# A normalisation chain in front of split-float32 matmuls, with its scale and its low parts moved to other engines

## The chip, the cores and the metric

The kernel runs on one core of one Trainium2 chip. The metric is the device time of one execution in microseconds, as the median of several runs.

## What is computed

The reference is two transformer blocks over 256 tokens with 256 context tokens and a model width of 1024, all in float32. Nearly every part begins with a root-mean-square norm, and in the first block the norm is modulated by a scale and a shift that come from a conditioning vector:

```python
def _rms_norm(x, gain):
    y = xf * lax.rsqrt(jnp.mean(xf * xf, axis=-1, keepdims=True) + EPS)
    return (y * gain.astype(jnp.float32)).astype(x.dtype)

def _modulated_norm(h, gain, shift, scale):
    return _rms_norm(h, gain) * (1.0 + scale) + shift

def _swiglu(h, w1, w2):
    a, b = jnp.split(h @ w1, 2, axis=-1)
    return (jax.nn.silu(a) * b) @ w2
```

The first block has two layers, each with an MLP, a mixer (delta rule, then window attention) and a second MLP, so it has six modulated norms. The second block has a plain norm with a gain in front of its three branches, one in front of its cross attention and one in front of its MLP.

## The kernel before

Everything is feature-major: a tile of 128 features lies across the partitions and the tokens lie along the free dimension (512 for context and latent tokens together, 256 for the latent ones alone). `KT` is 8, the number of feature tiles `d` of the model width.

A float32 product is made of three matmuls over split operands: weight and activation are each split into a high part (rounded to `fp32r`) and a low part (the rest), and `three` (lines 229 to 234) multiplies high by low (L232), low by high (L233) and high by high (L234) into one PSUM bank. Weights stream in units of eight 128x128 tiles: SyncE starts the load into one of three landing slots, ScalarE copies the high part (`feed_act`, L215), and GpSimd subtracts to get the low part (`feed_pool`, L225), both into one of four slots. TensorE waits for a unit's low part before its first tile.

The activations of a norm are split in the same way. The sum of squares is made on TensorE (L430), ScalarE takes the root (L459), VectorE the reciprocal `rr` (L493), and `spread_pe` (L470) spreads `rr` over the partitions into PSUM bank 5, followed by a fixed number of matmuls that nobody reads (`busy_pe`, L421: 14 rows in the trace for 512 tokens, 8 for 256). Then, for each feature tile `d`:

- VectorE, `norm_x_dve` (L499): work = residual x bank 5, all tokens in one instruction;
- ScalarE, `norm_act` (L486): high part = scale x work + shift, one instruction for each part of the tokens. A modulated norm over 512 tokens has two parts of 256, since context and latent tokens have their own scale and shift; every other norm has one part of 256;
- VectorE, `norm_z_dve` (L505): work = scale x work + shift, in place and in float32, by part, once the high part of that tile has been made (it overwrites what ScalarE reads);
- GpSimd, `norm_pool` (L521): low part = work - high part, all tokens in one instruction.

`norm_dve` interleaves the VectorE steps: it runs two tiles ahead with L499 and then alternates. The first matmuls of the next stage take the tiles in the order of `d`: `linear` waits for the low part of tile `d` and then runs `first` output tiles on it (two in an MLP, so six matmuls for each `d`; four in the second block's `glu` and `up2`, so twelve). The order on every engine is written out by hand in `pe_program`, `act_program`, `dve_program` and `pool_program`; each engine runs its list in order, and an instruction waits on a counter of another engine (`PE`, `AC`, `DV`, `PO`).

The norms are called, in order: `norm00` (before `mlp00`, at the start of the kernel, where L499 runs before the modulation scale has been made), `norm01` (before the delta projections), `norm02` (before `mlp01`), `norm10` (before `mlp10`), `norm11` (before the window-attention projections), all of these over 512 tokens; `norm12` (before `mlp11`) over 256 tokens; and `norm mix`, `norm xattn` and `norm mlp` of the second block, with a gain and without a shift. In an MLP the first L365 matmuls follow the two output tiles of `first`, so their start marks the end of the part of the matmuls that is fed by the norm.

## Time and profile before

| | |
|---|---|
| time, median of 3 runs | 2927.93 us (2921.97 to 2930.43) |
| the profiled execution: its own time | 2923.75 us |
| the profiled execution: its span | 2921.6 us |
| instructions | 51936 |
| TensorE busy | 2781.6 us, 95% of the span |
| VectorE busy | 1533.2 us, 52% |
| ScalarE busy | 1188.2 us, 41% |
| GpSimd busy | 1532.1 us, 52% |
| mean granted clock of TensorE | 0.978 |
| HBM read | 373.34 MB |

The span runs from the first to the last instruction of the profiled execution; the rest of its time, 2.15 us, lies around it. The profile's timeline merges instructions of one line that follow each other, so that a row's second number is the time from the start of the first to the end of the last of them. PE is TensorE, DVE is VectorE, ACT is ScalarE, POOL is GpSimd.

### The profile page before, as it was taken

The page shows a single profiled execution, that of the slowest core. Times are in us where ns is not written, and L with a number is a line of the kernel's source. Part 1 is how long each engine was busy: PE and PEld are TensorE (multiplying, and loading weights), DVE is VectorE, ACT ScalarE, POOL GpSimd, SP SyncE. Part 2 cuts the span into 40 slices and gives each one's busy share as a digit, 9 for nine tenths or more (in the row PEclk, how much of TensorE's full clock was granted, in tenths as well). Part 3 has the DMA queues.
Part 4 walks back from the last instruction along what each step waited for, and adds up shares of the span by engine and source line. Part 5 has one row for each costly group of instructions (what it writes and reads, how often), then busy time and mean ns, then how long its engine had stood idle before and what let it go on. Part 6 is the DMA issues. An engine that isn't in the chain of part 4 may idle for free.

```text
span 2921.6 us, 51936 instructions
## 1 busy us (share of the span) xinstructions
PE 2781.6 (95%) x21510; PEld 2393.9 (82%) x21510; DVE 1533.2 (52%) x2800; ACT 1188.2 (41%) x2083; POOL 1532.1 (52%) x857
## 2 busy tenths in 40 slices
PE   7999999988889999999999998899998999998999
PEld 5888877767777788887888885799997888997999
DVE  3777236645554666416665136453285765723570
ACT  3222235434453322223222245544455465545553
POOL 4444444443324544445444451488883665686797
PEclk8999999999999999999999999999998999999999
DMA  6565323210001555323554326265552433353365
GB/s 256 191 214 188 109 66 101 89 59 3 4 3 51 177 174 182 130 95 132 189 174 162 96 81 116 73 195 189 170 191 95 131 124 117 115 166 123 130 193 162
DMA packets 105969, 380.89 MB, mean 130 GB/s; under 512 B 11367, under 2 KB 16648, under 8 KB 104456
## 3 DMA queue, kind: packets, MB, share of 16 engines
q1 hardware_dynamic: 87304, 310.47, 33.0%
q10 hardware_dynamic: 18432, 67.12, 6.6%
q8 instruction: 171, 2.80, 0.4%
q14 instruction: 62, 0.51, 0.1%
HBM read 373.34 MB, written 4.19 MB: 129 GB/s over the span
## 4 chain that ended last, share of the span: by engine, by line
PE 84%; DVE 6%; POOL 3%; ACT 3%; issue 2%; DMA 1%; SPq 0%; ACTq 0%; DVEq 0%
PE bank L232 23%; PE bank L233 23%; PE bank L234 23%; POOL weights_lo L225 2%; PE bank L828 1%; DVE norm_work L505 1%; PE upper_banks L232 1%; PE upper_banks L233 1%; PE upper_banks L234 1%; DVE norm_work L499 1%; DMA ada_first<-w_ada 1%; DVE square_sums L452 1%; PE upper_banks L1564 1%; PE bank L1555 1%; PE bank L925 1%
## 5 line engine op out<-in xcount | busy, mean ns | idle before, releaser
L225 POOL TENSOR_TENSOR weights_lo<-weights_landing,weights_hi 128x1024 fp32r<-128x1024 f32 x554 | 1336.8, 2419 | 1116.5 <-ACT weights_hi L215 1116.0
L215 ACT ACTIVATE weights_hi<-weights_landing 128x1024 fp32r<-128x1024 f32 x554 | 586.6, 1061 | 1223.8 <-PE bank L234 1099.8
L232 PE MATMUL bank<-normed_hi,weights_lo 128*128 128x512 f32 (+1 forms) x2664 | 912.7, 343 | 16.9 <-POOL normed_lo L521 11.8
L233 PE MATMUL bank<-normed_lo,weights_hi 128*128 128x512 f32 (+1 forms) x2664 | 902.8, 339 | 0.0
L234 PE MATMUL bank<-normed_hi,weights_hi 128*128 128x512 f32 (+1 forms) x2664 | 902.1, 339 | 0.0
L232 PEld LDWEIGHTS bank<-normed_hi,weights_lo 128*128 128x128 f32 x2664 | 504.6, 189 | 101.2 <-POOL normed_lo L521 27.1
L234 PEld LDWEIGHTS bank<-normed_hi,weights_hi 128*128 128x128 f32 x2664 | 504.4, 189 | 61.4
L233 PEld LDWEIGHTS bank<-normed_lo,weights_hi 128*128 128x128 f32 x2664 | 504.8, 189 | 59.4
L232 PE MATMUL bank<-hidden_hi,weights_lo 128*128 128x512 f32 (+1 forms) x960 | 329.6, 343 | 0.0
L233 PE MATMUL bank<-hidden_lo,weights_hi 128*128 128x512 f32 (+1 forms) x960 | 329.4, 343 | 0.0
L234 PE MATMUL bank<-hidden_hi,weights_hi 128*128 128x512 f32 (+1 forms) x960 | 328.8, 343 | 0.0
L573 DVE TENSOR_TENSOR hidden_lo<-silus,hidden_hi 128x512 fp32r<-128x512 f32 (+1 forms) x88 | 210.8, 2395 | 87.4 <-ACT hidden_hi L560 87.4
L626 DVE SCALAR_TENSOR_TENSOR residual<-bank,gate,residual 128x256 f32<-128x256 f32 x80 | 35.5, 479 | 358.4 <-PE bank L234 358.4
L234 PEld LDWEIGHTS bank<-hidden_hi,weights_hi 128*128 128x128 f32 x960 | 180.2, 188 | 24.3
L233 PEld LDWEIGHTS bank<-hidden_lo,weights_hi 128*128 128x128 f32 x960 | 180.2, 188 | 24.2
L232 PEld LDWEIGHTS bank<-hidden_hi,weights_lo 128*128 128x128 f32 x960 | 180.1, 188 | 24.2
L391 DVE CUSTOM_DVE_ANT_0 ada_products<-ada_rows,upper_banks,k_cond_pack 128x1024 f32<-128x1024 f32 x128 | 163.3, 1276 | 21.0 <-DMA ada_rows<-w_ada_rows 11.8
L391 DVE CUSTOM_DVE_ANT_0 ada_rows<-ada_rows,upper_banks,k_cond_pack 128x1024 f32<-128x1024 f32 x128 | 163.1, 1274 | 0.0
L571 DVE TENSOR_TENSOR silus<-silus,bank 128x512 f32<-128x512 f32 (+1 forms) x88 | 54.6, 621 | 185.5 <-PE bank L234 160.5
L1746 DVE SCALAR_TENSOR_TENSOR upper_banks<-gl,k_pack,upper_banks 128x255 f32<-128x255 f32 (+14 forms) x240 | 113.5, 473 | 8.2
L521 POOL TENSOR_TENSOR normed_lo<-norm_work,normed_hi 128x512 fp32r<-128x512 f32 (+1 forms) x72 | 76.7, 1069 | 77.3 <-DVE norm_work L505 77.0
L452 DVE TENSOR_TENSOR square_sums<-square_sums,squares 128x512 f32<-128x512 f32 (+1 forms) x48 | 67.2, 1400 | 36.0 <-ACT squares L444 36.0
(442 smaller groups left out, 3800.9 us busy)
## 6 DMA issues: line engine op xcount, KB each, us to landing
weights_landing<-w_up SPq DMA_DIRECT2D x176, 512.0 KB, 3.5
ada_rows<-w_ada_rows ACTq DMA_DIRECT2D x128, 512.0 KB, 4.3
weights_landing<-w_down SPq DMA_DIRECT2D x88, 512.0 KB, 3.5
weights_landing<-w_dn SPq DMA_DIRECT2D x33, 512.0 KB, 3.4
weights_landing<-w_mlp_up SPq DMA_DIRECT2D x32, 512.0 KB, 3.5
weights_landing<-w_mlp_down SPq DMA_DIRECT2D x32, 512.0 KB, 3.5
weights_landing<-w_gate SPq DMA_DIRECT2D x24, 512.0 KB, 3.4
weights_landing<-w_xbc SPq DMA_DIRECT2D x24, 512.0 KB, 3.5
```

The source lines that it names most:

```text
L215: k.nc.scalar.activation(k.WH[:, u % SLOTS, :], k.W[:, u % LANDS, :], ACT.Copy).then_inc(*k.AC.mark(("unit hi", u)))
L225: k.nc.gpsimd.tensor_tensor(k.WL[:, u % SLOTS, :], k.W[:, u % LANDS, :], k.WH[:, u % SLOTS, :].bitcast(F32), ALU.subtract).then_inc(*k.PO. ...
L232: nc.tensor.matmul(out, ll, rh, start=start, stop=False, skip_group_check=True)
L233: nc.tensor.matmul(out, lh, rl, start=False, stop=False, skip_group_check=True)
L234: return nc.tensor.matmul(out, lh, rh, start=False, stop=stop, skip_group_check=True)
L391: nc.vector.tensor_tensor_reduce(k.row[r % ROW_LANDS][:] if c else k.row_out[:], k.row[r % ROW_LANDS][:], k.upper[:, c * D:(c + 1) * D], 1 ...
L452: k.nc.vector.tensor_tensor(s, s, k.sq[:, d % 2, 0:tokens], ALU.add).then_inc(*k.DV.mark((st, "sum", d)))
L521: k.nc.gpsimd.tensor_tensor(lo(d), work(d), hi(d).bitcast(F32), ALU.subtract).then_inc(*k.PO.mark((st, "lo", d)))
L571: nc.vector.tensor_tensor(s, s, k.B[(2 * p + 1) % 4][:, 0:tokens], ALU.mult).then_inc(*k.DV.mark((st, "raw", p)))
L573: nc.vector.tensor_tensor(lo(p), s, hi(p).bitcast(F32), ALU.subtract).then_inc(*k.DV.mark((st, "lo", p)))
L626: nc.vector.scalar_tensor_tensor(x, k.B[n % 4][:, a - first:b - first], gate(n, c), x, ALU.mult, ALU.add).then_inc(*k.DV.mark(*([(st, "ev" ...
L1746: nc.vector.scalar_tensor_tensor(y[:, a:LAT], x[:, 0:LAT - a], w[:, at, j:j + 1], y[:, a:LAT], ALU.mult, ALU.add).then_inc(*k.DV.mark(("co ...
```

## The change

In every norm the scale moves from the second and third step into the first: `norm_scaled_dve` (L498 of the changed kernel) makes work = (residual x scale) x bank 5 with one `scalar_tensor_tensor` for each part of the tokens. ScalarE makes the high part as work + shift, one part as soon as that part of work is there. The in-place step L505 of before is gone.

In the six modulated norms VectorE makes the low part too (`norm_low_dve`, L505 of the changed kernel): low = (work + shift) - high, by part, again one `scalar_tensor_tensor`, and the matmuls wait for VectorE (`norm_ready`). GpSimd only waits there until the last low part is made, and then goes on with its weights. In the three norms of the second block GpSimd still makes the low part, and now waits for ScalarE's high part alone. `norm_dve` now runs one tile ahead instead of two. In `norm00` all steps come after the scale.

```diff
-def norm_act(k, act, st, work, hi, parts, when=None):
+def norm_act(k, act, st, work, hi, parts):
     for d in range(KT):
-        act.wait_ge(*k.DV.after(st, "x", d))
         for n, (a, b, scale, shift) in enumerate(parts):
-            k.nc.scalar.activation(hi(d)[:, a:b], work(d)[:, a:b], ACT.Identity, scale=scale(d),
-                                   bias=shift(d) if shift else 0.0).then_inc(*k.AC.mark(*([(st, "hi", d)] if n == len(parts) - 1 else [])))
+            act.wait_ge(*k.DV.after(st, "scaled", d, n))
+            k.nc.scalar.activation(hi(d)[:, a:b], work(d)[:, a:b], ACT.Identity,
+                                   bias=shift(d) if shift else 0.0).then_inc(*k.AC.mark((st, "hi", d, n)))
...
-def norm_x_dve(k, dve, st, d, src, work, tokens, bank=5):
+def norm_scaled_dve(k, dve, st, d, src, work, parts, bank=5):
     if d == 0:
         dve.wait_ge(*k.PE.after(st, "spread"))
-    k.nc.vector.tensor_tensor(work(d), src(d), k.B[bank][:, 0:tokens], ALU.mult).then_inc(*k.DV.mark((st, "x", d)))
-def norm_z_dve(k, dve, st, d, work, parts):
-    dve.wait_ge(*k.AC.after(st, "hi", d))
     for n, (a, b, scale, shift) in enumerate(parts):
-        k.nc.vector.tensor_scalar(work(d)[:, a:b], work(d)[:, a:b], scale(d), shift(d) if shift else None, ALU.mult,
-                                  *((ALU.add,) if shift else ())).then_inc(*k.DV.mark(*([(st, "z", d)] if n == len(parts) - 1 else [])))
+        k.nc.vector.scalar_tensor_tensor(work(d)[:, a:b], src(d)[:, a:b], scale(d), k.B[bank][:, a:b], ALU.mult,
+                                         ALU.mult).then_inc(*k.DV.mark((st, "scaled", d, n)))
+def norm_low_dve(k, dve, st, d, work, hi, lo, parts):
+    for n, (a, b, scale, shift) in enumerate(parts):
+        dve.wait_ge(*k.AC.after(st, "hi", d, n))
+        k.nc.vector.scalar_tensor_tensor(lo(d)[:, a:b], work(d)[:, a:b], shift(d), hi(d)[:, a:b].bitcast(F32), ALU.add,
+                                         ALU.subtract).then_inc(*k.DV.mark(*([(st, "lo", d)] if n == len(parts) - 1 else [])))
...
     norm_r_dve(k, dve, st, tokens)
-    for d in range(KT + 2):
+    for d in range(KT + 1):
         if d < KT:
-            norm_x_dve(k, dve, st, d, src, work, tokens, bank)
-        if d >= 2:
-            norm_z_dve(k, dve, st, d - 2, work, parts)
+            norm_scaled_dve(k, dve, st, d, src, work, parts)
+        if d and st in MODULATED:
+            norm_low_dve(k, dve, st, d - 1, work, hi, lo, parts)
+MODULATED = ("norm00", "norm01", "norm02", "norm10", "norm11", "norm12")
+def norm_ready(k, st):
+    return lambda d: (k.DV if st in MODULATED else k.PO).after(st, "lo", d)
 def norm_pool(k, pool, st, work, hi, lo):
+    if st in MODULATED:
+        pool.wait_ge(*k.DV.after(st, "lo", KT - 1))
+        return
     for d in range(KT):
-        pool.wait_ge(*k.DV.after(st, "z", d))
+        pool.wait_ge(*k.AC.after(st, "hi", d, 0))
         k.nc.gpsimd.tensor_tensor(lo(d), work(d), hi(d).bitcast(F32), ALU.subtract).then_inc(*k.PO.mark((st, "lo", d)))
...
     norm_r_dve(k, dve, "norm00", TOK)
     ada_dve(k, dve, 1)
-    for d in range(KT):
-        norm_x_dve(k, dve, "norm00", d, src, work, TOK)
     for u in range(2, ADA_FIRST):
         ada_dve(k, dve, u)
+    dve.wait_ge(*k.DV.after("ada scale", 0, 0))
     for d in range(KT):
-        norm_z_dve(k, dve, "norm00", d, work, modulated(k, 0, 0))
+        norm_scaled_dve(k, dve, "norm00", d, src, work, modulated(k, 0, 0))
+        if d:
+            norm_low_dve(k, dve, "norm00", d - 1, work, hi, lo, modulated(k, 0, 0))
+    norm_low_dve(k, dve, "norm00", KT - 1, work, hi, lo, modulated(k, 0, 0))
```

The order of VectorE's instructions at the beginning of `norm01`, before:

```order
L493 RECIPROCAL rr<-rms 128x4 [waits act_done]
L499 TENSOR_TENSOR norm_work<-residual,upper_banks 128x512 [waits pe_done]
L499 TENSOR_TENSOR norm_work<-residual,upper_banks 128x512 x2
L505 TENSOR_SCALAR norm_work<-norm_work,scale,mod 128x256 [waits act_done]
L505 TENSOR_SCALAR norm_work<-norm_work,scale,mod 128x256
L499 TENSOR_TENSOR norm_work<-residual,upper_banks 128x512
L505 TENSOR_SCALAR norm_work<-norm_work,scale,mod 128x256 [waits act_done]
```

and of the changed kernel at the same place (`norm_work`, `normed_hi` and `normed_lo` hold work, high and low part; x2, x3 are repeats):

```order
L491 RECIPROCAL rr<-rms 128x4 [waits act_done]
L498 SCALAR_TENSOR_TENSOR norm_work<-residual,scale,upper_banks 128x256 [waits pe_done]
L498 SCALAR_TENSOR_TENSOR norm_work<-residual,scale,upper_banks 128x256 x3
L505 SCALAR_TENSOR_TENSOR normed_lo<-norm_work,mod,normed_hi 128x256 [waits act_done] x2
L498 SCALAR_TENSOR_TENSOR norm_work<-residual,scale,upper_banks 128x256 x2
```

The last three rows of before (one L499 on 512 tokens, two L505) repeat until the eighth tile; in the changed kernel the last two rows (two L505, two L498) do. Four L498 now stand ahead of the first low part, and both halves of it wait for ScalarE.

At the start of the kernel VectorE's order around `norm00` was (L346 makes the scale of the first norm, L571 is the first instruction of `mlp00`):

```order
L493 RECIPROCAL rr<-rms 128x4
L499 TENSOR_TENSOR norm_work<-residual,upper_banks 128x512 x8
L332 TENSOR_TENSOR mod<-upper_banks,k_cond_pack 128x2x4x2 x2
L346 SCALAR_TENSOR_TENSOR scale<-mod,k_cond_pack 128x16
L505 TENSOR_SCALAR norm_work<-norm_work,scale,mod 128x256 x16
L571 TENSOR_TENSOR silus<-silus,bank 128x512
```

and is now:

```order
L491 RECIPROCAL rr<-rms 128x4
L332 TENSOR_TENSOR mod<-upper_banks,k_cond_pack 128x2x4x2 x2
L346 SCALAR_TENSOR_TENSOR scale<-mod,k_cond_pack 128x16
L498 SCALAR_TENSOR_TENSOR norm_work<-residual,scale,upper_banks 128x256 x4
L505 SCALAR_TENSOR_TENSOR normed_lo<-norm_work,mod,normed_hi 128x256 x2
L498 SCALAR_TENSOR_TENSOR norm_work<-residual,scale,upper_banks 128x256 x2
```

The eight products of L499 stood ahead of the scale; the products of L498 need it and stand behind it.

## Rows read from the trace of the kernel before

**Rows 1.** The page: busy time of each engine, and the ended-last chain by line

```profile
PE 2781.6 (95%) x21510; PEld 2393.9 (82%) x21510; DVE 1533.2 (52%) x2800; ACT 1188.2 (41%) x2083; POOL 1532.1 (52%) x857
...
PE bank L232 23%; PE bank L233 23%; PE bank L234 23%; POOL weights_lo L225 2%; PE bank L828 1%; DVE norm_work L505 1%; PE upper_banks L232 1%; PE upper_banks L233 1%; PE upper_banks L234 1%; DVE norm_work L499 1%; DMA ada_first<-w_ada 1%; D
```

**Rows 2.** Windows: us, then busy time (and count) by engine, PEclk, DMA share, GB/s

```profile
940.00:959.00 19.00, 16.84 (x68) 11.57 (x68) 15.23 (x25) 10.33 (x18) 12.17 (x9) 1.00 0.00 1
959.00:1322.00 363.00, 362.69 (x1572) 291.81 (x1571) 180.44 (x229) 97.47 (x118) 156.63 (x66) 1.00 0.46 154
```

**Rows 3.** Timeline of VectorE in norm02: start us, us, engine, line, operation

```profile
940.93 1.88 DVE L499 TENSOR_TENSOR norm_work<-residual,upper_banks 128x512 f32<-128x512 f32 x3 [0.74 <-PE upper_banks L470]
...
942.79 0.73 DVE L505 TENSOR_SCALAR norm_work<-norm_work,scale,mod 128x256 f32<-128x256 f32 x2
...
944.04 1.31 DVE L505 TENSOR_SCALAR norm_work<-norm_work,scale,mod 128x256 f32<-128x256 f32 x2
...
945.86 1.33 DVE L505 TENSOR_SCALAR norm_work<-norm_work,scale,mod 128x256 f32<-128x256 f32 x2
```

**Rows 4.** Timeline of TensorE in norm02

```profile
940.73 3.19 PE L421 MATMUL upper_banks<-k_cond_pack 128*128 128x256 f32 x14
...
944.93 0.50 PE L232 MATMUL bank<-normed_hi,weights_lo 128*128 128x512 f32 x1 [1.01 <-POOL normed_lo L521]
...
957.41 0.50 PE L232 MATMUL bank<-normed_hi,weights_lo 128*128 128x512 f32 x1
...
958.91 1.91 PE L365 MATMUL upper_banks<-k_cond_pack,cond 128*128 128x128 f32 x16
```

**Rows 5.** Timeline of GpSimd in norm02

```profile
943.60 1.27 POOL L521 TENSOR_TENSOR normed_lo<-norm_work,normed_hi 128x512 fp32r<-128x512 f32 x1 [8.68 <-DVE norm_work L505]
```

**Rows 6.** Groups by line and shape: count | busy us, mean ns of one | idle before

```profile
L2269 DVE SCALAR_TENSOR_TENSOR mem<-mem,k_pack,upper_banks 128x256 f32<-128x256 f32 x8 | 3.2, 470 | 0.0
...
L499 DVE TENSOR_TENSOR norm_work<-residual,upper_banks 128x512 f32<-128x512 f32 x40 | 25.9, 679 | 3.9 <-PE upper_banks L470 3.9
...
L499 DVE TENSOR_TENSOR norm_work<-residual,upper_banks 128x256 f32<-128x256 f32 x32 | 12.5, 412 | 6.2 <-PE upper_banks L470 6.2
...
L486 ACT ACTIVATE normed_hi<-norm_work,mod,scale 128x256 fp32r<-128x256 f32 x88 | 46.2, 591 | 21.1 <-DVE norm_work L499 19.6 <-DVE scale L346 1.5
...
L486 ACT ACTIVATE normed_hi<-norm_work,k_pack 128x256 fp32r<-128x256 f32 x24 | 11.5, 506 | 9.7 <-DVE norm_work L499 9.7
...
L779 DVE SCALAR_TENSOR_TENSOR dn_g<-dn_ab_tmp,k_pack 128x64 f32<-128x64 f32 x1 | 0.2, 227 | 0.0
...
L772 DVE TENSOR_TENSOR dn_ab_tmp<-upper_banks,k_pack 128x64 f32<-128x64 f32 x1 | 0.2, 215 | 0.0
...
L2258 DVE TENSOR_TENSOR ssd_y_lo<-ssd_xbc,ssd_y_hi 128x256 fp32r<-128x256 f32 x16 | 14.6, 920 | 0.7 <-ACT ssd_y_hi L2237 0.6
```

**Rows 7.** Timelines of ScalarE and TensorE around norm00

```profile
38.02 7.98 ACT L486 ACTIVATE normed_hi<-norm_work,mod,scale 128x256 fp32r<-128x256 f32 x16 [1.54 <-DVE scale L346]
...
41.28 0.80 PE L232 MATMUL bank<-normed_hi,weights_lo 128*128 128x512 f32 x1 [3.72 <-POOL normed_lo L521]
...
54.37 1.91 PE L365 MATMUL upper_banks<-k_cond_pack,cond 128*128 128x128 f32 x16
```

**Rows 8.** Timelines of VectorE and TensorE in norm12: its first product, first matmul after

```profile
1880.31 1.08 DVE L499 TENSOR_TENSOR norm_work<-residual,upper_banks 128x256 f32<-128x256 f32 x3 [0.78 <-PE upper_banks L470]
...
1889.86 0.28 PE L232 MATMUL bank<-normed_hi,weights_lo 128*128 128x256 f32 x1
```

**Rows 9.** Timelines of TensorE in norm mix, and of GpSimd and TensorE around norm xattn

```profile
2074.72 0.39 PE L232 MATMUL bank<-normed_hi,weights_lo 128*128 128x256 f32 x1 [0.52 <-POOL normed_lo L521]
...
2637.80 0.74 POOL L521 TENSOR_TENSOR normed_lo<-norm_work,normed_hi 128x256 fp32r<-128x256 f32 x1 [0.23 <-DVE norm_work L505]
...
2644.82 7.05 POOL L225 TENSOR_TENSOR weights_lo<-weights_landing,weights_hi 128x1024 fp32r<-128x1024 f32 x3
...
2647.22 0.50 PE L232 MATMUL bank<-weights_hi,mem_lo 128*128 128x512 f32 x1 [2.39 <-POOL weights_lo L225]
```

More of the change, by code:

```diff
@@ L691, in delta_pe @@
     linear(k, pe, st, "w_dn", DN_TILES, KT, lambda d: (k.n_hi[:, d, :], k.n_lo[:, d, :]), TOK, freed,
-           lambda d: k.PO.after("norm01", "lo", d), first=2, beside=beside)
+           norm_ready(k, "norm01"), first=2, beside=beside)
 def delta_act(k, act):
@@ L1760, in glu_pe @@
     freed = lambda n: None if n < 8 else k.AC.after("glu", "sig", (n - 8) // 2) if n % 2 else k.DV.after("glu", "ev", (n - 8) // 2)
-    linear(k, pe, "glu", "w_glu", 2 * KT, KT, both2(k), LAT, freed, lambda d: k.PO.after("norm mix", "lo", d), first=4, banks=8)
+    linear(k, pe, "glu", "w_glu", 2 * KT, KT, both2(k), LAT, freed, norm_ready(k, "norm mix"), first=4, banks=8)
 def glu_act(k, act):
@@ L2519, in mlp2_pe @@
     freed = lambda n: k.DV.after("up2", "square", n - 8) if n >= 8 else None
-    linear(k, pe, "up2", "w_mlp_up", 4 * KT, KT, both2(k), LAT, freed, lambda d: k.PO.after("norm mlp", "lo", d), first=4, banks=8)
+    linear(k, pe, "up2", "w_mlp_up", 4 * KT, KT, both2(k), LAT, freed, norm_ready(k, "norm mlp"), first=4, banks=8)
     out_pe(k, pe, "down2", "w_mlp_down", 4 * KT, lambda d: (k.mh_hi[:, d, :], k.mh_lo[:, d, :]), LAT,
@@ L2675, in pe_program @@
     spread_pe(k, pe, "norm11", TOK)
-    window_project_pe(k, pe, swa, lambda d: k.PO.after("norm11", "lo", d), lambda n: None)
+    window_project_pe(k, pe, swa, norm_ready(k, "norm11"), lambda n: None)
     window_heads_pe(k, pe, swa)
@@ L2701, in pe_program, with norm_of_act @@
     mlp2_pe(k, pe)
-def norm_of_act(k, act, st, tokens, where, parts, when=None):
+def norm_of_act(k, act, st, tokens, where, parts):
     src, work, hi, lo = where
     rms_act(k, act, st, tokens)
-    norm_act(k, act, st, work, hi, parts, when)
+    norm_act(k, act, st, work, hi, parts)
 def act_program(k, act):
@@ L2712, in act_program @@
     start_act(k, act)
-    norm_act(k, act, "norm00", *first_norm(k, TOK)[1:3], modulated(k, 0, 0), k.DV.after("ada scale", 0, 0))
+    norm_act(k, act, "norm00", *first_norm(k, TOK)[1:3], modulated(k, 0, 0))
     mlp_act(k, act, "mlp00")
@@ L2750, in norm_of_dve @@
     src, work, hi, lo = where
-    norm_dve(k, dve, st, src, work, tokens, parts)
+    norm_dve(k, dve, st, src, work, hi, lo, tokens, parts)
 def dve_program(k, dve):
```

8 lines of the change are left out of this document (3 added, 5 removed).

## The prediction

> **What bounds the kernel now.** I read the page first. TensorE is busy for 95% of the span, and the chain that ended last is mostly its matmuls L232, L233 and L234; of the norms, L505 and L499 of VectorE appear in it with 1% each [rows 1]. So time can only be won where TensorE waits, and the next view, the busy time by windows, shows where: in the 363 us of `mlp01` TensorE is busy for 362.69, in the 19 us of the norm ahead of it for 16.84, much of that in matmuls that nobody reads [rows 2]. Both stretches have a granted clock of 1.00, which is the upper level, 2.4 GHz. The MLP's rate gives the price of a matmul on 512 tokens: 362.69 / 1572 = 0.231 us, so 1.4 us for the six that each feature tile feeds.
>
> The timelines of the three engines in `norm02` show what paces the feeding. I count from the first L499, at 940.93. VectorE runs three products in 1.88 us (0.60 from start to start), then two L505 in 0.73, and once GpSimd works beside it two L505 in 1.31 [rows 3]. One tile, a product and two L505, then takes VectorE 1.82 us (945.86 - 944.04) [rows 3], more than the 1.4 us of its matmuls. The filler matmuls end at 943.92 (2.99 after the start), the first low part at 944.87, and TensorE starts on it at 944.93, 0.06 later; the eighth tile's six matmuls run from 957.41 to 958.91, 1.50 us with their wait [rows 4, 5]. From the first product to the end of the fed part it is 17.98 us. `norm01`, `norm10` and `norm11` repeat this pattern, three more times.
>
> **The change, part by part, in a norm over 512 tokens.** VectorE now issues 32 `scalar_tensor_tensor` on 256 tokens: 16 products and 16 low parts. L2269 is the same operation with a per-feature scalar and one input in PSUM: eight back to back took 3.2 us, so 0.40 us from start to start, and 0.47 for one [rows 6]. That is the product's price. No row shows the low part's form, two large inputs in SBUF and a scalar, on 256 elements. A two-input product L499 on 256 elements costs 0.34 from start to start (three in 1.08, one 0.41) [rows 6, 8]; a low part of 256 elements from two inputs, L2258, costs 0.92 on average [rows 6]. I take 0.40, since L779, a `scalar_tensor_tensor` with both inputs in SBUF on 64 elements, takes 227 ns where the plain sum L772 takes 215 [rows 6]: the kind of input adds next to nothing. The bounds are 0.34 and 0.92.
>
> With 0.40 for both, the first tile's low part is VectorE's sixth instruction and ends at 5 x 0.40 + 0.47 = 2.47 us, ahead of the fillers' end at 2.99. So TensorE starts at 3.0 instead of 4.0. Then VectorE gives a tile every 1.60 us, still above 1.4. The seventh tile's low part is the 30th instruction and ends at 29 x 0.40 + 0.47 = 12.07, the eighth's at 12.87. TensorE: 12.07 + 0.06 + 1.50 = 13.63, and 1.40 more for the eighth tile, which is ready: 15.03. Before it was 17.98, so a norm gains 2.95 us, and four gain **11.8 us**.
>
> ScalarE hides under this: one high part took 591 ns with scale and shift and 506 with a scale alone [rows 6]; with the shift alone I put it near 0.51, about 1.0 for a tile against VectorE's 1.60. The new waits of VectorE on each half are met: the high part of a tile is asked for after two further products. Behind such a wait stand the next tile's products, so a late ScalarE would stall everything; it has 0.6 us a tile to spare. GpSimd loses its eight low parts and waits instead; its next weights come at 12.9 instead of 16.4 after the first product, so nothing behind it (its low parts, and the loads that SyncE issues after them) is later.
>
> **norm00.** Its eight early products were hidden behind a wait for the scale; now they stand behind it. The first high part started at 38.02, the first matmul at 41.28, the fed part ended at 54.37 [rows 7]. Now the first product starts at 38.02, the first low part ends at 40.49, TensorE starts at 40.55, **0.7 us** earlier, and needs the same 13.09 us, since it is slower than VectorE here (last low part at 50.9).
>
> **norm12.** 256 tokens, one part. From first product to the end of the fed part: 1889.86 - 1880.31 = 9.55 [rows 8]. Now the first low part waits for product (0.47) and high part (0.51), with 0.05 at each handing over: it starts at 1.08. Each tile then takes 0.80, more than the 0.70 of its six half-size matmuls; the seventh low part ends at 6.35, TensorE needs 0.06 + 0.80 + 0.70 for the last two tiles: 7.91. The gain is **1.6 us**.
>
> **The three plain norms.** L505 goes out of the path. In `norm mix` TensorE waits 0.52 us for the first low part and is the slower one afterwards [rows 9]; a step of some 0.4 us leaves the chain, **0.4 us**, and the same in `norm mlp`, **0.4 us**. In `norm xattn` GpSimd's eight low parts take from 2637.80 to 2644.82, and TensorE stands still for 2.39 us until the weights behind them are split [rows 9]. Without the waits for L505 they take 8 x 0.74 = 5.92 and start 0.23 earlier: **1.3 us**.
>
> The sum is 11.8 + 0.7 + 1.6 + 0.4 + 0.4 + 1.3 = **16.2 us**. Against the profiled execution's 2923.75 (span 2921.6 and 2.15 around it) that makes 2907.6. The median of the runs shown is 4.2 above that execution, and the forecast is for a median: 2927.93 - 16.2 = **2911.7**. If the low part costs only 0.34, TensorE bounds the norms (2.99 + 8 x 1.40, and 0.2 for waits, 14.4), and the sum is 19.0.
>
> **Rivals.**
> *A: the low part streams at half rate.* One element costs (679 - 412) / 256 = 1.04 ns [rows 6], so 256 more of them make a low part 0.67. Then the eighth tile is ready at 16 x 0.40 + 15 x 0.67 + 0.74 = 17.19 and the part ends at 18.75, +0.77 in each of four norms; `norm00` becomes bound by VectorE and ends at 56.8, +2.4; `norm12` +0.2; the plain norms still give 2.1. Together +3.6: 2931.5. Against it: on 64 elements half rate would add 67 ns, and L779 is 12 above L772 [rows 6]. For it: that is one row, on few elements. Chance 0.12. The Trainium skill, Vector Engine (DVE) Microarchitecture Reference, section "Points that are easy to get wrong", states such a rule: "`S2S2D2_STT` with two non-bf16 SBUF sources halves throughput"; this is the form of every new low part. By that rule the time is this rival's.
> *B: the low part meets GpSimd.* If GpSimd worked on SBUF during the low parts, they would cost like L2258, 0.92. The norm turns into a loss from 0.62 on (16 x 0.40 + 16 x 0.62 + 1.6 = 17.98). At 0.92 the part ends at 22.7, +4.7 in four norms, +6.3 in `norm00`, +2.2 in `norm12`, less 2.1: +25.2, 2953.1. For it: L505 went from 0.73 to 1.31 a pair when GpSimd started [rows 3]. Against it: GpSimd had been idle for 8.68 us before its first low part [rows 5], and now it is told to wait until VectorE's last. Chance 0.05. The Trainium skill, SBUF — State Buffer, section "Who interferes with whom", says that a VectorE instruction with two SBUF inputs contends with a GpSimd instruction that reads SBUF; the new wait of GpSimd is what that rule asks for.
> *C: waits break VectorE's overlap.* If each low part, being behind a wait, starts only when the instruction before has ended, 16 starts lose 0.07 each. A 512-token norm then gains 1.9, `norm12` 1.1, the sum is 11.4: 2916.5. Against it: a round of before, with one wait in it, is the 0.60 of its product and some 1.24 of its L505 pair, with nothing left over [rows 3]. Chance 0.10.
>
> **How the numbers follow.** My forecast has 0.71, C 0.10, A 0.12, B 0.05, and 0.02 is for what I have not seen. A measurement of this kernel can tell 0.3%, 8.8 us, from no change. Forecast and C lie beyond that (16.2 and 11.4), with 0.04 taken off for a median that comes out high: faster 0.77. A is the same, with that 0.04 and part of the unseen: 0.18. B is slower: 0.05. The range runs from the lowest run shown less the largest sum, 2921.97 - 19.0 = 2903.0, to the highest run less C's sum without the plain norms, 2930.43 - 9.3 = 2921.1. It leaves out A and B.
>
> **What the profile of the changed kernel would show.** L498 and the new L505 at 0.47 us each or less, 0.40 from start to start; in `norm02` the filler rows run straight into the first L232, and L365 starts 15.0 us after the first product instead of 18.0; no idle time of L505 on ScalarE beyond the first tile of `norm12`; no L521 in the first block. L505 near 0.74 would be A, far above it with GpSimd busy B. I am wrong if L365 comes less than 1 us earlier, or if it does and the total does not follow, which would mean that a later stage waits for something that doesn't move with the norm.

## The result and the profile after

The changed kernel takes 2909.93 us (median of 6 executions, 2901.82 to 2913.49), the kernel before 2924.72 on the same chip (6 executions, 2919.43 to 2930.43). The ratio is 0.9946, with a 95% interval from 0.9927 to 0.9965: faster by 0.54%, some 15.8 us (the two medians lie 14.8 apart). 2911.7 was forecast, and a gain of 16.2. The profiled execution took 2910.77 us (span 2908.6), 13.0 less than that of before.

The page of the changed kernel, its first part (busy us, share of the span, instructions), and the chain that ended last by engine. These lines answer to [rows 1]:

```profile
PE 2787.6 (96%) x21510; PEld 2402.9 (83%) x21510; DVE 1497.4 (51%) x2816; ACT 1180.2 (41%) x2083; POOL 1473.1 (51%) x809
...
PE 87%; DVE 4%; POOL 3%; ACT 3%; issue 2%; DMA 1%; SPq 0%; ACTq 0%; DVEq 0%
```

TensorE's share goes from 95 to 96% with the same 21510 matmuls, and GpSimd has 48 instructions fewer, the low parts of six norms. L505 and L499, each 1% of the chain before, are gone from the part of the chain's list by line that the page prints.

Busy time by windows, of `norm02` and of `mlp01` behind it (us from the start, then busy us and instructions of each engine, granted clock of TensorE, DMA share, GB/s). They answer to [rows 2]:

```profile
935.00:954.00 19.00, 18.87 (x90) 14.49 (x89) 12.87 (x33) 11.96 (x22) 5.15 (x3) 1.00 0.09 27
954.00:1314.00 360.00, 359.69 (x1551) 289.03 (x1550) 180.00 (x229) 94.63 (x116) 153.49 (x64) 1.00 0.46 154
```

In 19 us TensorE is now busy for 18.87 instead of 16.84. Behind the norm nothing changed: 359.69 / 1551 = 0.232 us a matmul (0.231 before), and from the end of `norm02`'s fed part to the first product of `norm10` it is 364.42 us (364.41 before). So what the norm gave was not asked back by the MLP.

The timeline of `norm02` (start us, us, engine, line, operation). VectorE and ScalarE answer to [rows 3], TensorE and GpSimd to [rows 4, 5]:

```profile
935.88 3.19 PE L421 MATMUL upper_banks<-k_cond_pack 128*128 128x256 f32 x14
936.08 1.66 DVE L498 SCALAR_TENSOR_TENSOR norm_work<-residual,scale,upper_banks 128x256 f32<-128x256 f32 x4 [0.74 <-PE upper_banks L470]
...
939.23 0.88 DVE L505 SCALAR_TENSOR_TENSOR normed_lo<-norm_work,mod,normed_hi 128x256 fp32r<-128x256 f32 x2
940.02 0.87 DVE L498 SCALAR_TENSOR_TENSOR norm_work<-residual,scale,upper_banks 128x256 f32<-128x256 f32 x2
940.53 0.91 ACT L484 ACTIVATE normed_hi<-norm_work,mod 128x256 fp32r<-128x256 f32 x2 [0.67 <-DVE norm_work L498]
940.81 0.88 DVE L505 SCALAR_TENSOR_TENSOR normed_lo<-norm_work,mod,normed_hi 128x256 fp32r<-128x256 f32 x2
...
947.11 1.67 DVE L505 SCALAR_TENSOR_TENSOR normed_lo<-norm_work,mod,normed_hi 128x256 fp32r<-128x256 f32 x4
...
948.85 7.09 POOL L225 TENSOR_TENSOR weights_lo<-weights_landing,weights_hi 128x1024 fp32r<-128x1024 f32 x3 [18.78 <-DVE normed_lo L505]
950.95 1.91 PE L365 MATMUL upper_banks<-k_cond_pack,cond 128*128 128x128 f32 x16
```

VectorE runs without a gap, one tile every 1.58 us (940.81 - 939.23) instead of 1.82. ScalarE idles 0.67 us in each round and waits for the product, not the other way round. L365, the end of the fed part, comes 950.95 - 936.08 = 14.87 us after the first product instead of 17.98.

The groups of instructions that the prediction priced (busy us, mean ns of one, idle time before them and what ended it), which answer to [rows 6]:

```profile
L484 ACT ACTIVATE normed_hi<-norm_work,mod 128x256 fp32r<-128x256 f32 x88 | 39.8, 502 | 30.8 <-DVE norm_work L498 30.8
L505 DVE SCALAR_TENSOR_TENSOR normed_lo<-norm_work,mod,normed_hi 128x256 fp32r<-128x256 f32 x88 | 38.4, 479 | 0.4 <-ACT normed_hi L484 0.4
L498 DVE SCALAR_TENSOR_TENSOR norm_work<-residual,scale,upper_banks 128x256 f32<-128x256 f32 x88 | 38.0, 475 | 3.8 <-PE upper_banks L470 3.8
...
L484 ACT ACTIVATE normed_hi<-norm_work 128x256 fp32r<-128x256 f32 x24 | 8.9, 413 | 2.5 <-DVE norm_work L498 2.5
```

The low part, with two inputs in SBUF, costs 479 ns; the product, with one of them in PSUM, 475. Over all 88 low parts VectorE waited 0.4 us for ScalarE.

Laid side by side, the stretches from each norm's first product to the end of what it feeds (in `norm xattn`, to the end of the first unit of weights that it feeds; in `norm00`, from the start of L346, which makes the scale, to L365):

| stretch | before, us | predicted gain | after, us | gain |
|---|---|---|---|---|
| norm01, 02, 10, 11 | 17.93 to 17.98 | 2.95 each, 11.8 | 14.84 to 14.87 | 3.1 each, 12.4 |
| norm12 | 9.55 | 1.6 | 7.93 | 1.6 |
| norm mix | 13.88 | 0.4 | 13.10 | 0.8 |
| norm xattn | 19.27 | 1.3 | 17.57 | 1.7 |
| norm mlp | 13.92 | 0.4 | 13.10 | 0.8 |
| norm00, from the scale | 16.56 | 0.7 | 16.50 | 0.1 |

That is 17.4 us. One row varies with the execution: six profiles have the changed kernel's opening unaltered (this one, e0_again, e1_plain_undone, e5_pool_free, e6_heads_filled and e9_heads_fitted), and in them `norm00` takes 15.3 to 16.8 us from the scale, 16.1 on average; of the kernel before there is one profile.

The position of the norms' reciprocals shows where the profiled execution lost part of it: `norm mix` comes 14.3 us earlier than before, `norm xattn` only 7.9. Between them lie 557.31 us before and 563.70 after.

### The profile page after: what moved, and what is told of

Its sections match the earlier page's. It is cut to its first block, busy times and chain, and to the rows that moved or that the text cites. A ratio compares the mean times of both kernels' runs of the same rounds, so it can differ in the third digit from the quotient of the medians.

```text
span 2908.6 us, 51910 instructions
## 1 busy us (share of the span) xinstructions
PE 2787.6 (96%) x21510; PEld 2402.9 (83%) x21510; DVE 1497.4 (51%) x2816; ACT 1180.2 (41%) x2083; POOL 1473.1 (51%) x809
## 4 chain that ended last, share of the span: by engine, by line
PE 87%; DVE 4%; POOL 3%; ACT 3%; issue 2%; DMA 1%; SPq 0%; ACTq 0%; DVEq 0%
PE bank L232 24%; PE bank L233 23%; PE bank L234 23%; POOL weights_lo L225 2%; PE bank L839 2%; PE upper_banks L233 1%; PE upper_banks L232 1%; PE upper_banks L234 1%; PE upper_banks L1575 1%; PE upper_banks L1590 1%; DMA ada_first<-w_ada 1%; DVE square_sums L452 1%; PE bank L1566 1%; PE bank L936 1%; PE upper_banks L421 1%
## 5 line engine op out<-in xcount | busy, mean ns | idle before, releaser
L225 POOL TENSOR_TENSOR weights_lo<-weights_landing,weights_hi 128x1024 fp32r<-128x1024 f32 x554 | 1337.6, 2421 | 1231.2 <-ACT weights_hi L215 1139.8
L232 PE MATMUL bank<-normed_hi,weights_lo 128*128 128x512 f32 (+1 forms) x2664 | 911.5, 342 | 6.9 <-POOL weights_lo L225 3.3
L232 PEld LDWEIGHTS bank<-normed_hi,weights_lo 128*128 128x128 f32 x2664 | 503.8, 189 | 83.8 <-DVE normed_lo L505 9.8
L232 PE MATMUL bank<-hidden_hi,weights_lo 128*128 128x512 f32 (+1 forms) x960 | 329.4, 343 | 0.0
L584 DVE TENSOR_TENSOR hidden_lo<-silus,hidden_hi 128x512 fp32r<-128x512 f32 (+1 forms) x88 | 203.1, 2308 | 88.3 <-ACT hidden_hi L571 88.3
L232 PEld LDWEIGHTS bank<-hidden_hi,weights_lo 128*128 128x128 f32 x960 | 180.1, 188 | 24.2
L632 DVE TENSOR_TENSOR residual<-residual,bank 128x256 f32<-128x256 f32 x24 | 9.8, 416 | 130.6 <-PE bank L234 130.6
```

The lines of the kernel that those rows point to most:

```text
L225: k.nc.gpsimd.tensor_tensor(k.WL[:, u % SLOTS, :], k.W[:, u % LANDS, :], k.WH[:, u % SLOTS, :].bitcast(F32), ALU.subtract).then_inc(*k.PO. ...
L232: nc.tensor.matmul(out, ll, rh, start=start, stop=False, skip_group_check=True)
L584: nc.vector.tensor_tensor(lo(p), s, hi(p).bitcast(F32), ALU.subtract).then_inc(*k.DV.mark((st, "lo", p)))
```

## The experiments

**The changed kernel again.**

> The changed kernel as it is, on another chip or at another time. In its first profile the nine norms won 18.9 us together, while the stretch between norm mix and norm xattn was longer by 6.4 us than before, with TensorE's granted clock in the attention heads there at 0.71 instead of 0.86. Theory 1 (chance of one execution): the fed part of norm02 is 14.9 us again, and the attention stretch comes out within 2 us of before's 541 us, clock there above 0.8. Rival (an earlier arrival of the heads costs them the clock each time): the stretch is again 5 us or more longer, clock near 0.7. Ratio to the kernel before 0.9946 +- 0.002 for both.

2907.58 us, ratio 0.9942 (0.9924 to 0.9960). The four norms take 14.83 to 14.87 us again, but from `norm mix` to `norm xattn` it is now 555.63 us. So the 6.4 us that the first profile lost there come and go with the execution. That stretch takes 555.6 to 557.7 us in four of the eight profiles of kernels with changed norms and nothing added to the heads, and 563.7 to 565.2 in the other four. The kernel before was profiled once, at 557.3, so whether the earlier arrival makes the longer one likelier isn't shown; but the mean granted clock of its 20 executions here varies as much, from 0.972 to 0.984. (The 18.9 us that the expectation gives the nine norms are 17.4 by the table.)

**The plain norms as before**: product without the gain, the gain again as ScalarE's scale, and L505's own step ahead of GpSimd.

```diff
-scalar_tensor_tensor(work, src, scale, B, mult, mult)
+tensor_tensor(work, src, B, mult)                       # three plain norms
+tensor_scalar(work, work, scale, None, mult)
```

> The changed kernel with the three plain norms of the second block as before (product, high part with scale on ScalarE, L505-like product in place, low part on GpSimd). Prediction's theory: each of norm mix and norm mlp gets back its 0.4 us and more (13.1 to 13.9 us from first product to the end of the fed part), norm xattn 1.3 to 1.7, so 3.3 us slower than the changed kernel, the modulated norms unchanged (14.9 in norm02). Rival (the plain norms were not on the path, their time was hidden by weights): under 1 us slower.

2911.15 us, ratio 0.9952 (0.9934 to 0.9970). The three stretches return to 13.86, 19.28 and 13.88 (13.88, 19.27 and 13.92 before the change), which gives back 3.25 us of the table's 3.3, and the modulated norms stay at 14.86. The total alone could not have told 3 us from nothing.

**Low parts back on GpSimd**, with the scale still in the product: VectorE adds the shift in place, GpSimd subtracts.

```diff
-scalar_tensor_tensor(lo, work, shift, hi, add, subtract)
+tensor_scalar(work, work, shift, None, add)             # VectorE
+tensor_tensor(lo, work, hi, subtract)                   # GpSimd
```

> The scale in the first product and the high part by half, but in the six modulated norms VectorE adds the shift in place and GpSimd makes the low part. Theory (VectorE's work per tile paces the norm, and it only falls with the fused low part): a tile costs 0.79 for its products and 0.66 to 1.24 for the two shifts beside GpSimd, about 2.0; fed part of norm02 18.5 to 19.6 us, no better than before's 17.98, total 1 to 4 us slower than before. Rival (the gain comes from the fused first product and the hand-over by half): fed part below 16.5, total at most 6 us slower than the changed kernel.

Its groups:

```profile
L529 POOL TENSOR_TENSOR normed_lo<-norm_work,normed_hi 128x512 fp32r<-128x512 f32 x40 | 52.0, 1299 | 55.4 <-DVE norm_work L505 55.1 <-DVE k_pack L1513 0.2
L505 DVE TENSOR_SCALAR norm_work<-norm_work,mod 128x256 f32<-128x256 f32 x88 | 47.9, 585 | 0.2 <-ACT normed_hi L484 0.2
```

2919.26 us, ratio 0.9983 (0.9968 to 0.9999). The stretch of `norm02` takes 17.40 us and a round 1.78. It had been put at 18.5 to 19.6, and the total at 1 to 4 us slower than before, so the direction was missed as well: the step beside GpSimd was priced like that of before, which has two scalars; with one it costs some 1.0 us a pair. Moving the scale, with the hand-over by half, brings 0.6 us of a norm's 3.1; the larger part comes with the low part's move.

**Low parts on VectorE, unfused**: product on 512 tokens, scale and shift in L510, difference in L516.

```diff
+tensor_scalar(work, work, scale, shift, mult, add)      # by half
+tensor_tensor(lo, work, hi, subtract)                   # 512 tokens, VectorE
```

> VectorE makes the low part, but in three kinds of instruction in the modulated norms: the plain product on 512 tokens, scale and shift in place by half, then the difference on 512 tokens; ScalarE applies scale and shift as before; GpSimd waits. Theory (VectorE's work per tile): 0.60 + 0.66 + 0.60 = 1.86 us a tile, fed part of norm02 17 to 18 us, so close to before's 17.98 and 2 to 3 us per norm behind the changed kernel. Rival (what pays is that GpSimd is out of VectorE's way and out of the chain): fed part 15.5 or less.

One round and a half in `norm02`, ScalarE's high parts among it:

```profile
951.06 0.91 DVE L510 TENSOR_SCALAR norm_work<-norm_work,scale,mod 128x256 f32<-128x256 f32 x2
951.88 0.68 DVE L499 TENSOR_TENSOR norm_work<-residual,upper_banks 128x512 f32<-128x512 f32 x1
952.48 0.68 DVE L516 TENSOR_TENSOR normed_lo<-norm_work,normed_hi 128x512 fp32r<-128x512 f32 x1
952.60 1.10 ACT L484 ACTIVATE normed_hi<-norm_work,mod,scale 128x256 fp32r<-128x256 f32 x2 [1.08 <-DVE norm_work L499]
953.23 0.91 DVE L510 TENSOR_SCALAR norm_work<-norm_work,scale,mod 128x256 f32<-128x256 f32 x2
```

2941.01 us, ratio 1.0051 (1.0030 to 1.0072): slower than before. GpSimd out of the way makes the pair of L510 cheaper (0.91, against 1.31 in [rows 3]), but the round is 2.17 us, and `norm02` takes 19.77; 1.86 and 17 to 18 were forecast. The forecast added up VectorE's starts alone. The rows show a loop through ScalarE instead: the product L499 ends at 952.56, ScalarE starts on its two halves at 952.60, the first is made 0.59 later, and L510 starts at 953.23; only one L516 stands between. VectorE is idle for 1.84 us of this norm, and the second L510 of a pair starts 0.49 after the first, where a pair that doesn't wait has 0.33 (the 0.73 for two in [rows 3]). The run therefore shows that the change of engine in this order costs 1.8 us a norm, and not that the unfused step must: with ScalarE out of the loop, an estimate from VectorE's starts is the 1.86 of the forecast (0.60 + 0.66 + 0.60), which is no better than the 1.82 of before. That the fusing, one pass for shift and difference, is what pays follows from that estimate and wasn't measured by itself. A fused low part on GpSimd wasn't tried either.

**GpSimd busy beside the new low parts**: after each product (one for each half) it adds two constant tiles of 128x256 into a spare buffer that nobody reads.

```diff
+pool.wait_ge(scaled d, n)
+tensor_tensor(spare, cond_pack[:, 0:256], cond_pack[:, 256:512], add)   # GpSimd, 88 in all
```

> The changed kernel with 16 sums of 128x256 from SBUF on GpSimd during each modulated norm (8 in norm12), one after each half product, into a spare buffer. Theory (rival B of the prediction: two large SBUF inputs meet GpSimd): L505 goes from 0.48 us to 0.9 or more while L498, with one input in PSUM, stays at 0.47; the fed part of norm02 grows from 14.9 to 19 us or more. Rival (no contention for this form): L505 stays below 0.6 and the fed part below 16.

Its groups, and two rows of its timeline in `norm02`:

```profile
L538 POOL TENSOR_TENSOR spare<-k_cond_pack 128x256 f32<-128x256 f32 x88 | 73.6, 837 | 48.7 <-DVE norm_work L499 36.9
L506 DVE SCALAR_TENSOR_TENSOR normed_lo<-norm_work,mod,normed_hi 128x256 fp32r<-128x256 f32 x88 | 60.3, 725 | 0.3 <-ACT normed_hi L485 0.2
```

```profile
948.49 1.35 DVE L506 SCALAR_TENSOR_TENSOR normed_lo<-norm_work,mod,normed_hi 128x256 fp32r<-128x256 f32 x2
949.76 0.86 DVE L499 SCALAR_TENSOR_TENSOR norm_work<-residual,scale,upper_banks 128x256 f32<-128x256 f32 x2
```

The low part goes from 479 to 725 ns, a pair from 0.88 to 1.35; the product, which reads PSUM beside SBUF, stays at 0.86 a pair. The stretch takes 18.61 to 18.63 us in all four norms, 3.8 more than in the changed kernel. There is one time of this kernel, 2933.41 us, beside a median of 2923.78 of before. Direction as expected, size smaller: 0.9 had been put for the low part, and 19 or more for the stretch.

**GpSimd not told to wait**, that is, its wait for the last low part left out.

```diff
-pool.wait_ge(lo, KT - 1)
```

> The changed kernel without GpSimd's wait for the last low part of a modulated norm, so that it may split weights during the norm. Theory: it finds nothing to split, since ScalarE's high parts of the weights come after its high parts of the norm and the weight slots are full; at most the last two low parts meet it; fed part of norm02 14.9 to 15.3 us, total the same within 1 us. Rival (the wait protects the low parts): L505 well above 0.48 on average, fed part 16 or more.

GpSimd's next weights in its `norm02`, which answers to the row at 948.85 of the changed kernel:

```profile
957.71 7.09 POOL L225 TENSOR_TENSOR weights_lo<-weights_landing,weights_hi 128x1024 fp32r<-128x1024 f32 x3 [18.70 <-ACT weights_hi L215]
```

2909.01 us, ratio 0.9947 (0.9931 to 0.9962), the four stretches 14.87, L505 483 ns. No difference: GpSimd starts on its weights 12.70 us after the first product, 12.77 with the wait, and is idle before them as long, now until ScalarE has made the weights' high part. Nothing of GpSimd's is ready to run earlier, so its wait costs nothing and guards against nothing in this order.

**Fillers where TensorE idles ahead of the second window's heads.** The stretch that varied holds the attention heads. In the changed kernel's profile TensorE's timeline has, ahead of them and at their start:

```profile
2216.62 0.61 PE L1363 MATMUL upper_banks<-k_pack,squares 128*128 128x2 f32 x4 [1.21 <-ACT rms L1470]
2217.20 0.66 PE L1373 MATMUL upper_banks<-k_cond_pack,rr 128*64 128x128 f32 x8
2219.03 1.12 PE L1373 MATMUL upper_banks<-k_cond_pack,rr 128*64 128x128 f32 x8 [1.17 <-DVE attn_q L1506]
2220.08 1.66 PE L1566 MATMUL bank<-attn_k,attn_q 64*128 64x128 f32 x8
2223.45 0.97 PE L1566 MATMUL bank<-attn_k,attn_q 64*128 64x128 f32 x4 [1.72 <-DVE attn_cols L1670]
```

The same eight L1373 take 0.66 us and, after two idle stretches, 1.12. Windows over the heads:

```profile
2230.00:2240.00 10.00, 9.66 (x51) 5.52 (x50) 6.25 (x32) 6.05 (x26) 0.00 (x0) 0.50 0.01 2
2240.00:2250.00 10.00, 9.66 (x51) 5.52 (x49) 5.67 (x28) 6.28 (x27) 0.00 (x0) 0.50 0.00 0
```

The granted clock is 0.50, 1.2 GHz, TensorE is busy for 97%, and a head takes 5.47 us. At 1.00 a head takes 4.28 and TensorE is busy for three quarters (the windows of e9_heads_fitted below). From the heads' start the lower level held for 15 us in the profile of before, and for 7 more in the last head, and for 53 us in the changed kernel's.

```diff
+busy_pe(k, 4, 0)    # ahead of the last sum of squares, and of the last spread
+busy_pe(k, 6, 4)    # after scores(0, 1), and after scores(1, 0)
```

> The changed kernel with 20 spare 128x256 matmuls of the identity in places where TensorE stood idle at the end of the second window projection and the start of its heads (4 before the last sum of squares, idle 1.21 us; 4 before the last spread, idle 1.17; 6 and 6 among the first scores, idle 1.72 and 1.66; a filler took 0.23 us at the full clock). Theory: the 6.4 us that the changed kernel's profile lost between norm mix and norm xattn are TensorE's clock and no part of the change: after these idle stretches the granted clock stood at the lower level, a head took 5.47 us instead of 4.28 and TensorE had no idle left in it. With the fillers the granted clock stays at 1.00 through the heads, the stretch from norm mix's to norm xattn's reciprocal takes 553 to 556 us (563.7 in the changed kernel's profile, 555.6 in its repeat, 557.3 before), and the median lies at 2901 to 2906. Rival: the clock falls there whatever the engine does, the fillers change nothing or cost 0 to 2 us, and the stretch takes 558 to 566 with the lower clock in the 20 us after the heads' start; median 2907 to 2912.

2900.13 us (2897.95 to 2904.62), ratio 0.9919 (0.9902 to 0.9935). The clock is 1.00 from 2200 to 2260. The stretch takes 556.9 us in this profile, not 553 to 556, and the median is a little below the forecast of 2901 to 2906. One filler is two matmul records and 0.46 us, not 0.23, so the twenty take 9.2 us in gaps of 5.8 (1.21 + 1.17 + 1.72 + 1.66) and overfill them by 3.4.

**Fillers in the opening.** `norm00` had shown 0.1 us of its 0.7 in the changed kernel's profile, and the timeline of TensorE there says why:

```profile
39.01 0.80 PE L232 MATMUL bank<-normed_hi,weights_lo 128*128 128x512 f32 x1 [2.96 <-DVE normed_lo L505]
39.60 0.63 PE L233 MATMUL bank<-normed_lo,weights_hi 128*128 128x512 f32 x1
...
44.30 0.51 PE L232 MATMUL bank<-normed_hi,weights_lo 128*128 128x512 f32 x1
44.64 0.40 PE L233 MATMUL bank<-normed_lo,weights_hi 128*128 128x512 f32 x1
```

From the scale to the first L232 it is 2.71 us, 0.76 less than before. But 12 matmuls start 0.43 apart or more, at the lower clock, against 8 before; four more at 0.2 each eat the gain. In the other five profiles with this opening the count is 14, 8, 11, 6 and 9, and `norm00` takes 16.79, 15.73, 16.27, 15.31 and 15.97 us from the scale, in the same order.

```diff
+busy_pe(k, 4, 4)    # ahead of each of the last two pieces of the modulation
+busy_pe(k, 9, 4)    # behind them, ahead of the first product
```

> The changed kernel with 17 spare matmuls in the opening: 4 before each of the last two pieces of the first modulation (TensorE idle 1.1 and 1.4 us there, waiting for their DMA) and 9 between the last of them and the first product with normed tokens (idle 2.96 us). Theory: norm00's gain of 0.76 us up to its first matmul was given back because TensorE began the products at the lower clock level and stayed there for 12 to 14 matmuls of 0.43 us in place of 9 before (0.23 us at the upper level). With the fillers the first products run at 0.23 to 0.25 us, and from the scale to the end of the fed part it takes 13.9 to 14.9 us in place of 16.3 to 16.5, since VectorE's round of 1.58 us for two tiles' six matmuls' pair then bounds it as in the other norms; the time falls by 1.5 to 2.4 us. Rival: the clock is at its lower level whatever is put there, the nine fillers take 0.46 each, 4.1 us in a gap of 2.96, and the time grows by about 1 us.

2906.02 us, ratio 0.9936 (0.9919 to 0.9953). The clock is 1.00 throughout the opening, and it takes 15.07 us from the scale to L365 instead of 15.3 to 16.8, though not the 13.9 to 14.9 expected: the fillers, too long here as well, made the first L232 0.7 us late. They also made the scale itself late. It starts to be made at 38.05 us, against 36.3 to 36.8 with the opening unaltered, so that L365 starts at 53.12, against 51.7 to 53.6. So the mechanism is shown in the trace, and counted from the kernel's start it gained nothing. The total, 1.6 us below the repeat of the changed kernel, can't be told from no change.

**Both sets.**

> Both sets of fillers on the changed kernel. Theory: the two gains add, 2899 to 2904 us, that is 0.2 to 0.35 per cent below the changed kernel, and the spread between executions narrows, since the stretch at the lower clock in the heads was its largest part. Rival: 2907 to 2912, no difference to the changed kernel.

2906.09 us (2900.33 to 2913.23), ratio 0.9939 (0.9920 to 0.9958). Both places look as in the single runs (1.00 at the clock, 15.07 us from the scale, 555.9 us between the norms), but the total isn't the 2899 to 2904 of the forecast, and the spread is no narrower. It is what the rival named, no difference to the changed kernel. See the last run.

**Both with half the fillers, first those of the heads alone** (2, 2, 3 and 3).

> As e6_heads_filled, with half the fillers (2, 2, 3 and 3): the trace showed that one 128x256 filler is two matmul records and 0.46 us, so that 4 and 6 of them took 1.85 and 2.8 us in gaps of 1.2 and 1.7, some 3.8 us too long in sum, while the granted clock stayed at 1.00 from 2200 to 2260 us. Theory: 0.92 and 1.4 us of fillers fit into the gaps and still keep the clock, so the stretch from norm mix's to norm xattn's reciprocal falls from 556.9 to 553 to 554.5 us and the median to 2895 to 2900. Rival: the clock stays up only because the long fillers left no idle at all; with 0.3 us left idle in each gap it falls again, the heads take 5.47 us each for a while, and the stretch takes 555 to 564 us, the median 2901 to 2910.

2898.86 us (2894.49 to 2903.55), ratio 0.9913 (0.9895 to 0.9930). Window and rows of its trace:

```profile
2220.00:2230.00 10.00, 7.64 (x52) 4.86 (x53) 7.90 (x41) 7.18 (x32) 0.00 (x0) 1.00 0.01 2
2230.00:2240.00 10.00, 7.28 (x63) 4.53 (x64) 7.60 (x37) 7.90 (x35) 0.00 (x0) 1.00 0.00 1
```

```profile
2217.63 1.56 PE L421 MATMUL upper_banks<-k_cond_pack 128*128 128x256 f32 x6
2220.61 0.67 PE L1570 MATMUL bank<-attn_k,attn_q 64*128 64x128 f32 x4 [1.42 <-DVE attn_cols L1678]
```

552.36 us from `norm mix` to `norm xattn`, 0.6 below the foot of the forecast, and 3.2 below the shortest of the profiles without fillers there. An idle stretch of 1.42 us was left and the clock stayed at 1.00.

**Then the opening's as well** (2, 2 and 6).

> As e9_heads_fitted, and in the opening 2 fillers before each of the last two pieces and 6 after them (0.9, 0.9 and 2.8 us for idle stretches of 1.1, 1.4 and 2.96). Theory: from the scale to the end of norm00's fed part 13.9 to 14.9 us (16.5 in the changed kernel, 15.07 with 9 fillers, which made the first product wait 0.8 us), so another 1.5 us less than e9_heads_fitted: 2893 to 2899. Rival: the clock at the first product is the lower one again, 16 to 17 us there, and the time is that of e9_heads_fitted.

2901.76 us (2896.92 to 2906.70), ratio 0.9921 (0.9902 to 0.9939). From the scale to L365 15.07 us, a little over the 14.9 expected, and L365 starts at 51.61 us, just below the lowest of the unaltered openings; from `norm mix` to `norm xattn` 551.08. Both parts do what they should, and yet the total is neither the 2893 to 2899 of the forecast nor below the run before it. The profile shows where this execution lost: from `norm01`'s to `norm02`'s reciprocal it took 529.3 us, against 518.4 in e9_heads_fitted. The delta heads lie there, and one of them met the lower clock in addition:

```profile
680.00:685.00 5.00, 4.43 (x66) 3.46 (x67) 4.81 (x18) 2.29 (x8) 3.26 (x10) 0.80 0.00 0
685.00:690.00 5.00, 4.98 (x41) 4.34 (x40) 1.64 (x4) 2.85 (x7) 4.09 (x10) 0.50 0.01 3
```

In the changed kernel both windows have 1.00. From the first to the last product of keys and queries (L886 of the changed kernel) the delta heads took 205.5 us before, 204.4 to 208.7 in eight of the nine changed kernels with the opening unfilled, 215.1 in the ninth, e5_pool_free, and 211.7, 212.2 and 214.5 in the three with a filled opening. So in both pairs (e6 and e8, e9 and e10) the fillers of the opening went with a longer total, not a shorter one. Whether they bring the longer delta heads on stays open: e5_pool_free had them without fillers, and no kernel but the changed one was profiled twice.

## Why the prediction was right, and where it was not

**The low part at 0.40.** Right, and on this all rested. It is 479 ns, and four instructions make a round of 1.575 us, 0.394 from start to start. Rival A, half rate, would have shown 0.74 and a round of 2.1 us or more. So the Trainium skill's rule (Vector Engine (DVE) Microarchitecture Reference, section "Points that are easy to get wrong"), that this form halves throughput with two sources in SBUF that aren't bfloat16, does not hold for these low parts: with two float32 sources in SBUF and with one of them in PSUM, the same operation differs by 4 ns on 256 elements.

**The four norms, 11.8.** 12.4. The forecast counted 29 starts of 0.40 to the seventh tile's low part; at 0.394 that is 0.17 us less a norm, which is the difference. That the fillers hold TensorE back until 2.99 was wrong: that is the end of their row, and the first normed matmul started 2.64 us after the first product, right behind the start of the last filler at 2.61, with the low part ready at 2.45. It changed nothing, since VectorE paces what follows.

**Rival B, GpSimd beside it.** Its mechanism is real and its size was too large: 0.725 instead of 0.92, measured with GpSimd kept busy, and the norm then takes 18.6, more than before. Only that GpSimd has nothing to do beside the new low parts keeps it away. This agrees with the Trainium skill (SBUF — State Buffer, section "Who interferes with whom") in both its halves: the low part with two inputs in SBUF is slowed, the product with one in PSUM isn't. The wait that GpSimd was given was credited with this and does nothing: without it the times are the same.

**Rival C, waits break the overlap.** Not so. Each half of a low part stands behind a wait, and in the four norms VectorE has no gap. Waits that are not yet met do break it, as in e3_low_on_dve_unfused.

**ScalarE hidden.** Right: 502 ns against 0.51 estimated, 0.67 us idle a round.

**norm00, 0.7.** The weak step is "TensorE ... needs the same 13.09 us". It began 0.76 us earlier as forecast, but in this profile it stayed at the lower clock for four more matmuls and took 13.8 us, so 0.1 remained. In the six profiles with this opening it took 12.6 to 14.1, which makes a gain of 0.5 on average (-0.2 to 1.2) against the one profile of before: the 0.7 is no worse than the spread, but the term held a quantity fixed that the clock moves by 1.5 us. With the clock held, this norm too is paced by VectorE, at 15.07 us.

**norm12, 1.6.** 7.93 for 7.91, with some luck in this profile: the fillers ahead of it ran mostly at the lower clock (a mean of 0.55 from the reciprocal to 2.55 us later), so the first matmul started at 2.08 instead of some 1.6, and TensorE then caught up at 0.70 a tile. In the repeat it started at 1.60 and followed VectorE at 0.79 a tile, as forecast, and the stretch is 7.83.

**The plain norms, 0.4, 1.3 and 0.4.** Sized too small: 0.8, 1.7 and 0.8. In `norm mix` 0.42 went out ahead of the first matmul, which was the term; the other 0.35 or so lies in the fed part, 11.66 us before and 11.31 after. It was taken for bound by TensorE from its second tile on, and was not quite: before, TensorE came to the fourth unit of weights at the seventh tile and lost 0.27 us there, from start to start, since GpSimd splits that unit (L225) only after its eight low parts and ended it 11.54 us after the reciprocal; now it ends at 9.67 and nothing is lost. This is the wait that the prediction had seen in `norm xattn`. The rest is the rate of the half-size matmuls, on which see the end. Undoing this part gave back 3.25 of the 3.3.

**The sum.** 17.4 from the stretches, 16.2 forecast, some 15.8 by the ratio. The difference between the stretches and the total lies within what the clock changes from one execution to the next (the changed kernel's executions at a mean clock of 0.972 took 2913, that at 0.982 took 2902). That the forecast of the sum comes within 0.4 us of the ratio's figure is luck at that spread: by the table `norm00` was too large by 0.6, the others together too small by 1.8.

## What to carry to other kernels

Price the engine that paces a pipeline by starts, not durations, and look for an arithmetic step that another instruction on the same data can take along: fused it brought 3.1 us a norm; unfused on the same engine, and with ScalarE's latency in the loop, it cost 1.8. Count also what another engine needs between an instruction and the one that waits for its result. A stretch can lose, at a lower TensorE clock, what a change gained elsewhere; so compare stretches between two marks before totals, and look at the granted clock of the stretch where the shift between two traces shrinks. Idle stretches of TensorE ahead of a stretch in which it is close to the bound at half clock are worth filling: here ten small matmuls brought some 0.3% (ratio 0.9913 after 0.9942), about half of what the change did. That figure is rough: the two intervals overlap a little, and over the four kernels with filled heads the ratio is 0.9913 to 0.9939.

## What the runs showed of the hardware beyond that

- TensorE's clock in the second window's attention heads was at its lower level from their start, for 15 to 53 us, in all nine profiles without fillers there; in the four with them it was at the upper one for seven of the eight heads at least (it fell in the last head of two). The engine had been idle for 1.2 us, ran two short groups, and was idle for 1.17 us more; the level fell within that second stretch in six of the nine profiles, and within 0.41 us behind it in the other three; with fillers it had 0.15 us or less idle at either place, and a later idle stretch of 1.42 us did not lower it. The best kernel, the change with ten fillers, takes 2898.86 us, 0.87% less than before.
- ScalarE's high part of 256 tokens costs 591 ns with scale and shift from memory [rows 6], 502 with one of them, 413 with neither: 89 ns for each.
- A pair of in-place steps on VectorE beside a busy GpSimd depends on its scalars: 1.31 with two [rows 3], 1.07 with one (e2_low_on_pool), for the same bytes. Ahead of GpSimd's start it is 0.73 with two [rows 3] and 0.61 with one.
- The half-size matmuls of `mlp11` and of the last MLP ran at either of two rates, at a granted clock of 1.00 both times: 48 of them take 5.60 or 5.65 us, the same rate throughout a stage. Over `mlp11` that is 1.7 us, and it ran at the slower rate in 5 of the 13 profiles; over the last MLP it is 1.5 us, slower in 6. Between the two profiles of before and after, `mlp11` went to the slower rate and the last MLP to the faster, so the sum hardly shows it: from the reciprocal of `norm mlp` to the end of the kernel it is 184.84 us before and 182.42 after, of which only 0.8 is the norm's. The cause is open.
